# Sums of squares on two column halves of the TensorE array, ahead of the two MLPs

## The chip, the cores and the metric

One core of a Trainium2 chip runs the whole program. The metric is the device time of one execution in microseconds (us). TensorE (PE) multiplies, VectorE (DVE), ScalarE (ACT) and GpSimd (POOL) work element by element, and SyncE and ACT issue most of the DMAs. The engines run side by side and meet at semaphores.

## The reference, cut to what matters

The program is a two-layer encoder trunk over 16 learned and 1024 given tokens (1040 in all) of width 1024. Each layer adds a mixer (RG-LRU and gated linear attention heads) and then an MLP, each of them with an RMSNorm before it and one behind it.

```python
def rmsnorm(x, g):
    y = xf * lax.rsqrt(jnp.mean(xf * xf, axis=-1, keepdims=True) + EPS)
    return y.astype(x.dtype) * g
...
for l in range(DEPTH):
    mix = hybrid_mixer(rmsnorm(h, norm_mix_pre[l]), ...)
    h = h + rmsnorm(mix, norm_mix_post[l])
    ff = squared_relu_mlp(rmsnorm(h, norm_mlp_pre[l]), w_mlp_up[l], w_mlp_down[l])
    h = h + rmsnorm(ff, norm_mlp_post[l])
```

The change is in how `mean(xf * xf)` of the RMSNorm ahead of the MLP (norm_mlp_pre) is summed over the 1024 features.

## The kernel before, in words

**Layout.** Activations lie with the features on the 128 partitions, in KT = 8 feature tiles, and the tokens along the free axis. Layer 0 works on 3 blocks of 348 tokens (`FULL`, the last block is 344 wide in the weight products), layer 1 behind the mixer on 2 blocks of 512 (`LAST`). A *piece* is two feature tiles of one block: 12 pieces of 2 x 348 columns in layer 0, 8 pieces of 2 x 512 in layer 1. Four pieces (QT) make a block.

**Products.** Weights and activations are split into a high and a low part of type fp32r, and each product is three passes: high x high, high x low, low x high. Sums over the partitions are plain fp32 products with a matrix of ones, so that every output partition holds the sum. An fp32 product shows in the trace as two records of MATMUL, an fp32r pass as one.

**Where the change sits.** Behind the mixer, `update(l, 0, ...)` makes the new residual piece by piece. DVE scales and adds (L2050, L2061), ACT writes the high part of the piece scaled by the gain (L1421, called x_hi below) and its squares, both feature tiles at once, into a ring of three (`sq`, L1426), and DVE writes the low part (L2021, called x_lo below). TensorE follows in `first_pair`, which multiplies the first two weight units of the MLP (jobs J_MLP and J_MLP+1) with the pieces as they come. For each piece it does the high passes (L865), then `add_piece`, the two fp32 products of the piece's squares with ones (L852, L853) into a sum bank, then the low passes (L870). In the last block the second unit's passes are put off in part: its feature tiles 4 to 7 come after the last piece, 8 high passes and 4 low ones.

**What follows.** When the last piece of a block is summed, ACT takes the logarithm out of the sum bank (`log_mean`, L1407) and an exponential (`inv_root`, L1414), which gives 1/rms in `rs`. The norm's scale is applied behind the product: DVE's relu (L2443) multiplies the up projection's banks by `rs` and so needs all blocks of it. Only that relu frees the bank set of job J_MLP (`ps_free`, 3 banks in layer 0, 2 in layer 1), and the third unit (`unit_job`, L808) waits for this set. The two sum banks alternate from block to block, and a block's first sum waits until ACT has read the sum two blocks back (`take_sum_bank`). The sum of the norm behind the mixer (`row_sum`, L992) stands after piece 2 in layer 0 and after piece 1 in layer 1. The order of all of it is written out by hand, the same in each engine's program, and semaphores count pieces and sums. `acc` is the tile in which DVE adds up the squares of the mixer's output; it is free once L992 has read it.

Of the kernel before, what the change touches and what calls it, by code (L numbers as in the profile page):

```python
# [21 lines left out]
D = 1024  # L22
N_META, SEQ = 16, 1024
NT = N_META + SEQ
NB, BN = 3, 348
# [75 lines left out]
NX, QT = NB * KT // 2, KT // 2  # L101
# [157 lines left out]
def trunk_kernel(nc, x_in, w_units, w_zg, w_gates, w_decay, params, h_out):  # L259
# [6 lines left out]
    with ctx:  # L266
# [3 lines left out]
        def sem(name):  # L270
            return ctx.enter_context(nc.semaphore(name))
# [174 lines left out]
        def sq(t, n):  # L446
            return sq_last[n % SQ_RING][:, :, :] if t is LAST else sq_full[:, n % SQ_RING]
# [5 lines left out]
        def stream(dram, n, t):  # L453

            m, b = piece(n)
            return dram[m:m + 2, :, t.first + b * t.bn:t.first + (b + 1) * t.bn].rearrange("k p n -> p k n")

        def sum_bank(l, norm, b):

            return banks[:, 6 + sum_index(l, norm, b) % 2, 0:of_norm(l, norm).bn]  # L460
# [13 lines left out]
        x_hi, x_lo = sem("x_hi"), sem("x_lo")  # L474
        sq_h, sq_added, sq_read = sem("sq_h"), sem("sq_added"), sem("sq_read")
        sum_done, sum_read = sem("sum_done"), sem("sum_read")
        rs_ready = sem("rs_ready")
        banks_zeroed, branch_end = sem("banks_zeroed"), sem("branch_end")
        pad_zeroed, conv_step, xc_ready = sem("pad_zeroed"), sem("conv_step"), sem("xc_ready")
# [322 lines left out]
        def _(pe):  # L802
# [38 lines left out]
            def add_piece(l, norm, n, sbase):  # L841

                t, b, first, last = of_norm(l, norm), n // QT, n % QT == 0, n % QT == QT - 1
                if first:
                    take_sum_bank(l, norm, b)
                if sbase == 0:
                    pe.wait_ge(sq_added, n + 1)
                    nc.tensor.matmul(sum_bank(l, norm, b), ones[:, :], sq(t, n)[:, 0, :], start=first, stop=last)\
                        .then_inc(sum_done if last else sq_read, 1)
                    return  # L850
                pe.wait_ge(sq_h, sbase + n + 1)
                nc.tensor.matmul(sum_bank(l, norm, b), ones[:, :], sq(t, n)[:, 0, :], start=first, stop=False)  # L852
                nc.tensor.matmul(sum_bank(l, norm, b), ones[:, :], sq(t, n)[:, 1, :], start=False, stop=last)\  # L853
                    .then_inc(sum_done if last else sq_read, 1)

            def first_pair(l, norm, unit, j, slots, xbase, sbase, last_sum):

# [4 lines left out]
                def hi_passes(u, b, k, parts=(0, 1)):  # L862
                    w, lead = wslot(slots[u], k), lead_of(u, b)
                    for n in parts:
                        nc.tensor.matmul(ps(j + u, t=t)[:, b, lead:t.width(b)], w[n], xtile(k)[0][:, b * t.bn + lead:b * t.bn + t.width(b)],  # L865
                                         start=k == 0 and n == 0, stop=False)
# [42 lines left out]
                for n in range(2 if sbase == 0 else 0, t.pieces):  # L909
                    m, b = piece(n)  # L910
                    late = b == t.nb - 1

                    lag = [k - QT for k in (m, m + 1) if k >= QT] if late else [m, m + 1]
                    if n == 0:
                        pe.wait_ge(w_ready, l * COUNTED_UNITS + unit + 3)
                        take_set(l, j)
                    pe.wait_ge(x_hi, xbase + n + 1)
                    for k in (m, m + 1):
                        hi_passes(0, b, k)
                    if n == 0:  # L920
                        pe.wait_ge(w_ready, l * COUNTED_UNITS + unit + 1 + 3)
                        take_set(l, j + 1)
                    for k in lag:
                        hi_passes(1, b, k)
                    add_piece(l, norm, n, sbase)
                    pe.wait_ge(x_lo, xbase + n + 1)
                    for k in (m, m + 1):
                        first = lo_pass(0, b, k)
                    if n == t.pieces - 1:
                        first.then_inc(mm_done, 1)  # L930
                    for k in lag:
                        lo_pass(1, b, k)
                    if n == (2 if t is FULL else 1) and last_sum:
                        row_sum(*last_sum)
                for k in range(QT, KT):
                    hi_passes(1, t.nb - 1, k)
                for k in range(QT, KT):
                    ins = lo_pass(1, t.nb - 1, k)
                ins.then_inc(mm_done, 1)
# [47 lines left out]
            def row_sum(l, phase, b):  # L987

                norm = POST_MIX + 2 * phase
                take_sum_bank(l, norm, b)  # L990
                pe.wait_ge(acc_done, total(adds, l, phase) + whole_adds(l, phase) + (b + 1) * per_block(l, phase))
                nc.tensor.matmul(sum_bank(l, norm, b), ones[:, :], acc[:, projected_tokens(l, phase).cols(b)], start=True, stop=True)\  # L992
                    .then_inc(sum_done, 1)
# [409 lines left out]
        def _(act):  # L1403
            def log_mean(l, norm, b):

                act.wait_ge(sum_done, sum_index(l, norm, b) + 1)
                nc.scalar.activation(rs[:, of_norm(l, norm).cols(b)], sum_bank(l, norm, b), ACT.Ln, scale=1.0 / D, bias=eps[:, 0:1])\  # L1407
                    .then_inc(sum_read, 1)

            def inv_root(l, norm, b):  # L1410

# [14 lines left out]
                nc.scalar.activation(sq(t, n), Y[:, m:m + 2, t.cols(b)], ACT.Square).then_inc(sq_h, 1)  # L1426

            def last_sum(l, norm):
                log_mean(l, norm, of_norm(l, norm).nb - 1)
                inv_root(l, norm, of_norm(l, norm).nb - 1)  # L1430

# [35 lines left out]
            def update(l, phase, source, target):  # L1467
# [59 lines left out]
                if t is LAST:  # L1527
                    new_piece(1)
                    new_piece(2)
                    root(norm, 1)  # L1530
                    new_piece(3)
                    new_piece(4)
                    log_mean(l, norm + 1, 0)
                    new_piece(5)
                    new_piece(6)
                    inv_root(l, norm + 1, 0)
                    new_piece(7)
                else:
                    new_piece(1)
                    squares_of(2, first)  # L1540
                    if phase == 1:
                        root(norm, 1)
                        new_piece(2)
                    else:
                        new_piece(2)
                        root(norm, 1)
                    squares_of(2, second)
                    new_piece(3)
                    new_piece(4)
                    root(norm, 2)  # L1550
                    new_piece(5)
                    new_piece(6)
                    log_mean(l, norm + 1, 0)
                    for n in range(7, NX - 1):
                        new_piece(n)
                    log_mean(l, norm + 1, 1)
                    inv_root(l, norm + 1, 0)
                    inv_root(l, norm + 1, 1)
                    new_piece(NX - 1)

            for n in range(2):
                m, b = piece(n)
# [1278 lines left out]
```

## Time and profile before

| | us |
|---|---|
| median of 3 runs | 2210.37 (2210.19 to 2212.29) |
| the profiled execution, its own time | 2211.12 |
| its span in the trace | 2209.4 |
| TensorE busy in the span | 2186.9 (99%) |
| VectorE busy | 1640.6 (74%) |
| ScalarE busy | 899.8 (41%) |
| fp32 products with ones ahead of the MLPs | 40: 24 of 348 columns, 16 of 512 |

Busy times overlap, since the engines run side by side. The stretches with the pieces ahead of the MLPs are 433 to 472 us (layer 0) and 1539 to 1576 us (layer 1). A busy TensorE is one that has a product in flight; how closely the products follow each other is seen from the starts of their rows.

### The profile page before, as it was taken

What the parts mean: (1) busy time and instruction counts of PE and PEld (TensorE: products, weight loads), DVE (VectorE), ACT (ScalarE), POOL (GpSimd) and SP (SyncE); (2) the same over time, 40 slices, a digit from 0 to 9 for tenths busy, and PEclk for the clock granted to TensorE, in tenths of its full rate; (3) what the DMA queues carried; (4) which work ended last, traced back from release to release, by engine and by line L of the source; (5) the groups of instructions that cost most, each with busy time, mean ns of one, the idle gap of its engine ahead of it and who ended that gap; (6) DMA issues with size and microseconds to landing.
All of it is one profiled execution on the core that took longest, in us unless ns stands there. A gap on an engine that the chain in (4) does not pass through costs nothing.

```text
span 2209.4 us, 34577 instructions
## 1 busy us (share of the span) xinstructions
PE 2186.9 (99%) x13888; PEld 1990.1 (90%) x13888; DVE 1640.6 (74%) x1649; ACT 899.8 (41%) x1053; POOL 342.9 (16%) x195
## 2 busy tenths in 40 slices
PE   8999999999999999999999999999999999999998
PEld 7999989999999999999989999887788888888888
DVE  7788635576878877979687886354768779779897
ACT  4564424352433433333354653242524433433435
POOL 3333215112000000000313322151130000000000
PEclk9999999999999999999999999999999999999999
DMA  4111102255653654554341111022556544643744
GB/s 145 41 54 32 37 20 96 73 180 191 252 183 138 221 187 160 194 202 172 110 142 42 53 39 39 20 96 69 179 208 231 190 182 168 237 171 127 253 152 153
DMA packets 126928, 300.49 MB, mean 136 GB/s; under 512 B 9840, under 2 KB 29552, under 8 KB 126832
## 3 DMA queue, kind: packets, MB, share of 16 engines
q1 hardware_dynamic: 59568, 172.58, 21.9%
q10 hardware_dynamic: 67264, 126.55, 16.7%
q8 instruction: 70, 1.15, 0.2%
q14 instruction: 26, 0.21, 0.0%
HBM read 265.24 MB, written 33.85 MB: 135 GB/s over the span
## 4 chain that ended last, share of the span: by engine, by line
PE 87%; DVE 8%; ACT 2%; issue 2%; DMA 0%; POOL 0%; SPq 0%; DVEq 0%; ACTq 0%; POOLq 0%
PE banks L808 26%; PE banks L1142 23%; PE banks L1179 22%; PE banks L978 5%; PE banks L865 3%; DVE lr L2205 1%; PE banks L870 1%; PE banks L1279 1%; PE banks L853 1%; PE banks L852 1%; PE banks L1286 1%; PE banks L1256 1%; PE banks L1235 1%; PE banks L1294 1%; DVE xc L2234 1%
## 5 line engine op out<-in xcount | busy, mean ns | idle before, releaser
L808 PE MATMUL banks<-X,w_hl 128*128 128x348 f32 (+3 forms) x3264 | 556.9, 329 | 0.0
L808 PEld LDWEIGHTS banks<-X,w_hl 128*128 128x128 f32 x3264 | 522.8, 188 | 17.1 <-issue 3.0
L1142 PE MATMUL banks<-X,w_hl 128*128 128x260 f32 (+1 forms) x2268 | 363.4, 320 | 0.0
L1142 PEld LDWEIGHTS banks<-X,w_hl 128*128 128x128 f32 x2268 | 323.9, 188 | 34.1 <-DVE Y L2468 0.4
L1179 PE MATMUL banks<-sum_hi,w_hl 128*128 128x260 f32 (+1 forms) x1440 | 310.5, 320 | 0.0
L708 POOL TENSOR_SCALAR w_hl<-w_raw 128x1024 fp32r<-128x1024 f32 x59 | 69.5, 1178 | 1155.8 <-PE banks L1142 515.7
L1179 PEld LDWEIGHTS banks<-sum_hi,w_hl 128*128 128x128 f32 x1440 | 223.6, 188 | 21.1
L1179 PE MATMUL banks<-sum_lo,w_hl 128*128 128x260 f32 (+1 forms) x720 | 191.1, 320 | 0.0
L712 POOL TENSOR_TENSOR w_hl<-w_raw,w_hl 128x1024 fp32r<-128x1024 f32 x59 | 174.6, 2959 | 4.9
L1795 ACT ACTIVATE sum_hi<-hid 128x1040 fp32r<-128x1040 f32 (+1 forms) x72 | 76.8, 1066 | 200.1 <-PE banks L1179 200.1
L2537 DVE TENSOR_TENSOR Y<-banks,Y 128x520 f32<-128x520 f32 (+1 forms) x144 | 122.5, 872 | 21.6 <-PE banks L1179 20.8
L1179 PEld LDWEIGHTS banks<-sum_lo,w_hl 128*128 128x128 f32 x720 | 119.0, 188 | 10.6
L1761 ACT ACTIVATE w_hl<-r 128x1024 fp32r<-128x1024 f32 x76 | 80.2, 1055 | 113.5 <-PE banks L1179 55.2
L1179 PE MATMUL banks<-sum_hi,w_third 128*128 128x260 f32 (+1 forms) x576 | 125.7, 320 | 0.0
L1142 PE MATMUL banks<-X,w_third 128*128 128x260 f32 (+1 forms) x756 | 124.6, 321 | 0.1
L1142 PEld LDWEIGHTS banks<-X,w_third 128*128 128x128 f32 x756 | 108.4, 188 | 12.6 <-DMA X<-t_mem 1.3
L1776 ACT ACTIVATE hid<-banks 128x1040 f32<-128x1040 f32 (+1 forms) x56 | 57.9, 1033 | 143.4 <-PE banks L1142 143.2
L2485 DVE TENSOR_TENSOR w_hl<-w_raw,w_hl 128x1024 fp32r<-128x1024 f32 x52 | 63.6, 1223 | 52.4 <-ACT w_hl L1761 52.4
L2485 DVE TENSOR_TENSOR w_hl<-r,w_hl 128x1024 fp32r<-128x1024 f32 x76 | 92.7, 1220 | 7.2 <-ACT w_hl L1761 7.0
L1179 PEld LDWEIGHTS banks<-sum_hi,w_third 128*128 128x128 f32 x576 | 89.8, 188 | 8.4
L1780 ACT ACTIVATE hid<-hid 128x1040 f32<-128x1040 f32 (+1 forms) x56 | 59.9, 1069 | 91.1 <-DVE hid L2507 82.8
L2537 DVE TENSOR_TENSOR Z<-banks,Z 128x520 f32<-128x520 f32 (+1 forms) x108 | 91.7, 874 | 4.4 <-PE banks L1179 3.8
(271 smaller groups left out, 3706.9 us busy)
## 6 DMA issues: line engine op xcount, KB each, us to landing
w_raw<-w_units SPq DMA_DIRECT2D x142, 512.0 KB, 3.5
r<-w_units SPq DMA_DIRECT2D x88, 512.0 KB, 4.0
X<-t_mem ACTq DMA_DIRECT2D x52, 520.0 KB, 5.5
X<-t_mem ACTq DMA_DIRECT2D x52, 512.0 KB, 5.4
X<-t_mem SPq DMA_DIRECT2D x32, 520.0 KB, 5.6
X<-t_mem SPq DMA_DIRECT2D x32, 512.0 KB, 5.8
t_extra<-t_mem ACTq DMA_DIRECT2D x19, 520.0 KB, 4.4
t_extra<-t_mem ACTq DMA_DIRECT2D x19, 512.0 KB, 5.3
```

Of the source, the lines that this page charges most:

```text
L708: nc.gpsimd.tensor_scalar(slot[:, 0], w_raw[:, s], 1.0, 1.0, ALU.mult, ALU.mult).then_inc(w_rounded, 1)
L712: nc.gpsimd.tensor_tensor(slot[:, 1], w_raw[:, s], slot[:, 0].bitcast(f32), ALU.subtract).then_inc(w_ready, 1)
L808: ins = nc.tensor.matmul(out[:, b, lead:t.width(b)], wp, xp[:, b * t.bn + lead:b * t.bn + t.width(b)], start=first and n == 0, stop=last a ...
L865: nc.tensor.matmul(ps(j + u, t=t)[:, b, lead:t.width(b)], w[n], xtile(k)[0][:, b * t.bn + lead:b * t.bn + t.width(b)], start=k == 0 and n ...
L978: ins = nc.tensor.matmul(block_bank(j0, q)[:, 0:t.width(b)], wp, xp[:, t.used(b)], start=i == 0 and n == 0, stop=i == last_k and n == 2)
L1142: ins = nc.tensor.matmul(banks[:, first + b, 0:t.block], wp, xp[:, b * t.block:(b + 1) * t.block], start=opens and (half, kk, i) == (0, 0, ...
L1179: ins = nc.tensor.matmul(out[:, m + b, :], wp, xp[:, k, b * t.block:(b + 1) * t.block], start=k == 0 and i == 0, stop=k == 1 and i == 2)
L1761: nc.scalar.activation(wslots[W_SLOT[operand]][:, 0], r_first[:, :, :] if first else raws[raw], ACT.Copy).then_inc(wpart_hi, 1)
L1780: nc.scalar.activation(quarter(l, q), quarter(l, q), ACT.Square).then_inc(act_sq, 1)
L1795: nc.scalar.activation(sum_part(l, sum_hi, part), source, ACT.Copy).then_inc(xpart_hi, 1)
L2485: V.tensor_tensor(slot[:, 1], r_first[:, :, :] if first else raws[W_RAW[operand]], slot[:, 0].bitcast(f32), ALU.subtract).then_inc(wpart_r ...
L2537: ins = V.tensor_tensor(to, part_banks(l, job), to, ALU.add)
```

## The change

In `add_piece`, for the norm ahead of the MLP alone, the two products of a piece no longer use the whole array one after the other. Each uses 64 of its 128 columns (`ones[:, rows]`): the first feature tile's squares are summed into partitions 0 to 63 of the sum bank, the second tile's into partitions 64 to 127. When a block's four pieces are through, the bank holds two half sums. ACT copies it to `acc` (`copy_halves`), and TensorE adds the halves by a whole fp32 product with ones (`whole_sum`). Each of the two is then in it 64 times, which the scale of the logarithm takes out (`repeated`). In TensorE's program `whole_sum` of a block stands after piece 2 of the next block in layer 0 (pieces 6 and 10), after piece 1 of it in layer 1 (piece 5), and for the last block between the last 8 high and the last 4 low passes of the second unit. ACT's order is shifted to fit.

```diff
@@ add_piece (TensorE)
                 pe.wait_ge(sq_h, sbase + n + 1)
+                if norm == PRE_MLP:
+                    for half in range(2):
+                        rows = slice(64 * half, 64 * half + 64)
+                        ins = nc.tensor.matmul(sum_bank(l, norm, b)[rows], ones[:, rows], sq(t, n)[:, half, :], start=first, stop=last,
+                                               skip_group_check=True)
+                    ins.then_inc(halves_done if last else sq_read, 1)
+                    return
                 nc.tensor.matmul(sum_bank(l, norm, b), ones[:, :], sq(t, n)[:, 0, :], start=first, stop=False)
                 nc.tensor.matmul(sum_bank(l, norm, b), ones[:, :], sq(t, n)[:, 1, :], start=False, stop=last)\
                     .then_inc(sum_done if last else sq_read, 1)
+
+            def whole_sum(l, norm, b):
+
+                pe.wait_ge(halves_copied, halves_before(l, norm, b) + 1)
+                nc.tensor.matmul(sum_bank(l, norm, b), ones[:, :], acc[:, of_norm(l, norm).cols(b)], start=True, stop=True).then_inc(sum_done, 1)
@@ first_pair (TensorE)
                     if n == (2 if t is FULL else 1) and last_sum:
                         row_sum(*last_sum)
+                    if norm == PRE_MLP and n % QT == (2 if t is FULL else 1) and n > QT:
+                        whole_sum(l, norm, n // QT - 1)
                 for k in range(QT, KT):
                     hi_passes(1, t.nb - 1, k)
+                if norm == PRE_MLP:
+                    whole_sum(l, norm, t.nb - 1)
                 for k in range(QT, KT):
                     ins = lo_pass(1, t.nb - 1, k)
@@ log_mean (ScalarE)
+                repeated = 64 if norm == PRE_MLP else 1
                 act.wait_ge(sum_done, sum_index(l, norm, b) + 1)
-                nc.scalar.activation(rs[:, of_norm(l, norm).cols(b)], sum_bank(l, norm, b), ACT.Ln, scale=1.0 / D, bias=eps[:, 0:1])\
+                nc.scalar.activation(rs[:, of_norm(l, norm).cols(b)], sum_bank(l, norm, b), ACT.Ln, scale=1.0 / (D * repeated), bias=eps[:, 0:1])\
                     .then_inc(sum_read, 1)
+
+            def copy_halves(l, norm, b):
+
+                act.wait_ge(halves_done, halves_before(l, norm, b) + 1)
+                nc.scalar.activation(acc[:, of_norm(l, norm).cols(b)], sum_bank(l, norm, b), ACT.Copy).then_inc(halves_copied, 1)
@@ last_sum (ScalarE)
+                if norm == PRE_MLP:
+                    copy_halves(l, norm, of_norm(l, norm).nb - 1)
                 log_mean(l, norm, of_norm(l, norm).nb - 1)
                 inv_root(l, norm, of_norm(l, norm).nb - 1)
@@ update, layer 1 (ScalarE)
                     new_piece(4)
-                    log_mean(l, norm + 1, 0)
+                    copy_halves(l, norm + 1, 0)
                     new_piece(5)
                     new_piece(6)
+                    log_mean(l, norm + 1, 0)
+                    new_piece(7)
                     inv_root(l, norm + 1, 0)
-                    new_piece(7)
...
```

TensorE's program at one piece of layer 0 (the first piece of the stretch; `w_out_87` and `w_out_88` are the slots of the first two weight units), before:

```order
L865 MATMUL banks<-X,w_out_88 128x348 x4
L852 MATMUL banks<-sq,ones 128x348
L853 MATMUL banks<-sq,ones 128x348
L870 MATMUL banks<-X,w_out_87 128x348 x2
L870 MATMUL banks<-X,w_out_88 128x348 x2
```

and after the change:

```order
L882 MATMUL banks<-X,w_out_88 128x348 x4
L860 MATMUL banks<-sq,ones 64x348 x2
L887 MATMUL banks<-X,w_out_87 128x348 x2
L887 MATMUL banks<-X,w_out_88 128x348 x2
```

The two whole products have become two of 64 columns; the passes on either side stand as they did.

TensorE's program at the end of the same stretch, from the last piece to the third unit (`w_hl`), before:

```order
L865 MATMUL banks<-X,w_out_88 128x344 x4
L852 MATMUL banks<-sq,ones 128x348
L853 MATMUL banks<-sq,ones 128x348
L870 MATMUL banks<-X,w_out_87 128x344 x2
L870 MATMUL banks<-X,w_out_88 128x344 x2
L865 MATMUL banks<-X,w_out_88 128x344 x8
L870 MATMUL banks<-X,w_out_88 128x344 x4
L808 MATMUL banks<-X,w_hl 128x348 x2
```

and after the change:

```order
L882 MATMUL banks<-X,w_out_88 128x344 x4
L860 MATMUL banks<-sq,ones 64x348 x2
L887 MATMUL banks<-X,w_out_87 128x344 x2
L887 MATMUL banks<-X,w_out_88 128x344 x2
L882 MATMUL banks<-X,w_out_88 128x344 x8
L871 MATMUL banks<-acc,ones 128x348
L887 MATMUL banks<-X,w_out_88 128x344 x4
L813 MATMUL banks<-X,w_hl 128x348 x2
```

The product that completes the last block's sum now stands behind 12 more passes than before (2 + 2 + 8), with 4 passes left behind it instead of 16.

ScalarE's program at the same place, from the high part of the last piece (piece 11), before:

```order
L1421 ACTIVATE X<-Y,par 128x348 x2
L1426 ACTIVATE sq<-Y 128x696
L1487 DMA h_mid<-Y 128x2x348
L1407 ACTIVATE rs<-banks,eps 128x348
L1414 ACTIVATE rs<-rs 128x348
L1906 ACTIVATE x_scaled<-Y,par 128x1040 x2
```

and after the change:

```order
L1448 ACTIVATE X<-Y,par 128x348 x2
L1453 ACTIVATE sq<-Y 128x696
L1516 DMA h_mid<-Y 128x2x348
L1429 ACTIVATE rs<-banks,eps 128x348
L1441 ACTIVATE rs<-rs 128x348
L1435 ACTIVATE acc<-banks 128x348
L1429 ACTIVATE rs<-banks,eps 128x348
L1441 ACTIVATE rs<-rs 128x348
L1951 ACTIVATE x_scaled<-Y,par 128x1040 x2
```

The logarithm and exponential of the middle block have moved behind the last piece, and the copy of the last block's half sums (`acc<-banks`) stands ahead of its logarithm.

## Rows read from the trace of the kernel before

**Rows 1.** The page: busy time by engine, and TensorE's granted clock in 40 slices.
```profile
PE 2186.9 (99%) x13888; PEld 1990.1 (90%) x13888; DVE 1640.6 (74%) x1649; ACT 899.8 (41%) x1053; POOL 342.9 (16%) x195
...
PEclk9999999999999999999999999999999999999999
```

**Rows 2.** The page: the chain that ended last, by engine.
```profile
PE 87%; DVE 8%; ACT 2%; issue 2%; DMA 0%; POOL 0%; SPq 0%; DVEq 0%; ACTq 0%; POOLq 0%
```

**Rows 3.** Timeline, PE, layer 0: start us, duration us, then the merged group.
```profile
437.07 1.44 PE L865 MATMUL banks<-X,w_out 128*128 128x348 f32 x8
...
440.16 1.44 PE L865 MATMUL banks<-X,w_out 128*128 128x348 f32 x8
```

**Rows 4.** Chain in order of time, one fp32 product of each layer: start us, us.
```profile
439.09 0.58 PE banks L853 x2
...
1571.65 0.86 PE banks L853 x2
```

**Rows 5.** Timeline, PE, two long rows of fp32r passes, one for each layer.
```profile
471.61 8.65 PE L808 MATMUL banks<-X,w_hl 128*128 128x348 f32 x53
...
1576.06 22.39 PE L808 MATMUL banks<-X,w_hl 128*128 128x512 f32 x96
```

**Rows 6.** Timeline, PE, the products on 32-column quarters (128*32), and what follows.
```profile
41.76 3.70 PE L1358 MATMUL banks<-Y,zg_w 128*32 128x348 f32 x48 [0.17 <-DVE xb L1963]
45.39 0.43 PE L808 MATMUL banks<-X,w_hl 128*128 128x348 f32 x1
```

**Rows 7.** Timeline, PE, into and out of products on 64-column halves (104*64).
```profile
249.22 0.80 PE L808 MATMUL banks<-X,w_hl 128*128 128x344 f32 x4
249.95 1.09 PE L1235 MATMUL banks<-v_tok,keys_t 104*64 104x128 f32 x16
250.98 0.64 PE L1223 MATMUL banks<-ident,ki 128*104 128x128 f32 x4
...
275.71 0.82 PE L1235 MATMUL banks<-v_tok,keys_t 104*64 104x128 f32 x12
276.46 1.71 PE L808 MATMUL banks<-X,w_hl 128*128 128x348 f32 x9
```

**Rows 8.** Timeline, PE, ACT and DVE, the end of layer 0's stretch.
```profile
466.49 1.41 PE L865 MATMUL banks<-X,w_out 128*128 128x344 f32 x8
467.74 0.75 PE L852 MATMUL banks<-sq,ones 128*128 128x348 f32 x2
...
469.11 0.56 ACT L1407 ACTIVATE rs<-banks,eps 128x348 f32<-128x348 f32 x1 [4.28 <-PE banks L853]
469.69 0.49 ACT L1414 ACTIVATE rs<-rs 128x348 f32<-128x348 f32 x1
...
470.22 2.64 DVE L2443 SCALAR_TENSOR_TENSOR T<-banks,rs 128x1044 f32<-128x1044 f32 x2 [4.96 <-ACT rs L1414]
```

**Rows 9.** Timeline, PE, ACT and DVE, the end of layer 1's stretch.
```profile
1568.79 2.00 PE L865 MATMUL banks<-X,w_out 128*128 128x512 f32 x8
1570.63 1.02 PE L852 MATMUL banks<-sq,ones 128*128 128x512 f32 x2
...
1572.55 0.69 ACT L1407 ACTIVATE rs<-banks,eps 128x512 f32<-128x512 f32 x1 [5.13 <-PE banks L853]
...
1573.93 1.23 DVE L2443 SCALAR_TENSOR_TENSOR T<-banks,rs 128x1024 f32<-128x1024 f32 x1 [6.01 <-ACT rs L1414]
```

**Rows 10.** Timeline, PE and DVE, inside layer 1's stretch, and one DVE row of layer 0.
```profile
1548.25 1.02 PE L992 MATMUL banks<-acc,ones 128*128 128x512 f32 x2
1561.18 1.09 PE L865 MATMUL banks<-X,w_out 128*128 128x512 f32 x4
...
1550.69 1.23 DVE L2050 TENSOR_TENSOR Y<-Y,rs 128x1024 f32<-128x1024 f32 x1 [1.50 <-ACT rs L1414]
1561.10 1.41 DVE L2021 SCALAR_TENSOR_TENSOR X<-Y,par,X 128x512 fp32r<-128x512 f32 x2
...
460.67 1.06 DVE L2021 SCALAR_TENSOR_TENSOR X<-Y,par,X 128x348 fp32r<-128x348 f32 x2
```

More of the change, by code:

```diff
@@ L456, in stream, with halves_before @@
             return dram[m:m + 2, :, t.first + b * t.bn:t.first + (b + 1) * t.bn].rearrange("k p n -> p k n")
+        def halves_before(l, norm, b):
+            return NB * l + b
         def sum_bank(l, norm, b):
@@ L476, in trunk_kernel @@
         sum_done, sum_read = sem("sum_done"), sem("sum_read")
+        halves_done, halves_copied = sem("halves_done"), sem("halves_copied")
         rs_ready = sem("rs_ready")
@@ L1550, in update @@
                     root(norm, 2)
[L1551 to L1559, printed above, removed]
+                    if phase == 0:
+                        new_piece(5)
+                        new_piece(6)
+                        copy_halves(l, norm + 1, 0)
+                        new_piece(7)
+                        new_piece(8)
+                        log_mean(l, norm + 1, 0)
+                        new_piece(9)
+                        new_piece(10)
+                        copy_halves(l, norm + 1, 1)
+                        inv_root(l, norm + 1, 0)
+                        new_piece(NX - 1)
+                        log_mean(l, norm + 1, 1)
+                        inv_root(l, norm + 1, 1)
+                    else:
+                        new_piece(5)
+                        new_piece(6)
+                        log_mean(l, norm + 1, 0)
+                        for n in range(7, NX - 1):
+                            new_piece(n)
+                        log_mean(l, norm + 1, 1)
+                        inv_root(l, norm + 1, 0)
+                        inv_root(l, norm + 1, 1)
+                        new_piece(NX - 1)
             for n in range(2):
```

## The prediction, made before the changed kernel ran

> **What bounds the kernel now.** I read the page's busy times first: TensorE is busy for 2186.9 of 2209.4 us at the full granted clock, the 2.4 GHz level, in every slice [rows 1], and the chain that ended last is 87% TensorE [rows 2]. So the change counts by what it does to TensorE's stream in two stretches of about 40 us, and by whether that stream must wait at their ends. The timeline of these stretches comes next. In layer 0 a piece takes 3.09 us, from 437.07 to 440.16 [rows 3]: 12 fp32r passes and two fp32 products. An fp32 product costs 0.585 us there and 0.86 in layer 1, by the steps of the chain [rows 4]. An fp32r pass costs (8.65 - 0.32) / 52 = 0.160 us in layer 0 and (22.39 - 0.40) / 95 = 0.231 in layer 1 (0.32 and 0.40 being one pass alone) [rows 5]; within the pieces 8 passes take 467.74 - 466.49 = 1.25, so 0.157 each [rows 8]. TensorE waits for nobody in the stretches. It is about to at their ends: in layer 0 the last sum is out at 469.1, ACT's two steps run to 470.2, DVE's first relu, half of 2.64 us or 1.25 alone, ends at about 471.47 [rows 8], and the third unit starts at 471.61 [rows 5]. That is sum to restart 2.5 us, and TensorE's own 16 passes behind that sum's stream (468.91 + 16 x 0.157) end just 0.2 us before it. In layer 1 DVE is through at 1573.93 + 1.23 = 1575.16 [rows 9], while TensorE's own passes last until 1576.06 [rows 5]: 0.9 us of slack.
>
> **What the change removes.** Two 64-column products side by side take the time of one. The trace has that: 16 records of 64-column products in 1.09 us [rows 7]. One after the other at the 0.109 us that a step has there (0.82 - 0.27 over 5 steps of the 12-record row) they would take 1.74; in pairs 0.87 and the latency. On quarters of the array and all 128 rows it holds too: 48 records in 3.70 us are 12 steps of 0.29 [rows 6]. So a piece saves 0.585 us (layer 0) or 0.86 (layer 1) before costs.
>
> **What a visit to the halves costs.** Going in: four whole passes from 249.22 at 0.157 end at 249.85, but the first pair starts at 249.95, 0.10 late, and the pairs then need 1.09 - 0.27 = 0.82 us for seven steps of 0.11, 0.05 too long [rows 7]. Coming out: the last pair of the 12-record row starts at 275.71 + 0.82 - 0.27 = 276.26, the next product is due at 276.37 and comes at 276.46, 0.09 late, and its nine passes take 1.71 where 8 steps of 0.16 and 0.32 make 1.60: 0.11 more. Together 0.35 us a visit. The quarters' exit agrees: 45.39 is 0.12 later than 41.76 + 12 x 0.2925, and the first pass lasts 0.43 instead of 0.32 [rows 6]. Bounds: 0.20 if the late entry was only a wait for data, 0.40 by the quarters' exit. I take 0.35, whose rows are of this very tile width.
>
> The Trainium skill, "TensorEngine Tiling (Array Packing)", Key Properties, says that changing the tiling mode drains TensorE; it gives no price. The trace agrees, with the 0.35 us above. The same page's Theoretical Speedup table gives up to 2x for two column halves; taken alone, without the drain, that is the second rival below.
>
> So a piece saves 0.585 - 0.35 = 0.235 us in layer 0 and 0.86 - 0.35 = 0.51 in layer 1.
>
> **What it adds.** Five whole products with ones (three of 0.585, two of 0.86) and five copies on ACT. A copy is priced by its nearest row, the logarithm out of the same bank, 0.56 or 0.69 us [rows 8, 9], between 0.5 and 0.8. ACT is 41% busy [rows 1] and each copy is made long before it is wanted. The tightest is the last: the copy is there 0.6 us after the half sums, and TensorE has 12 passes (1.9 us) in between. So the copies cost nothing; without that cover each would cost its 0.6.
>
> **Layer 0, step by step.** When the last piece starts TensorE is ahead by 11 x 0.235 less two whole sums, 2.59 - 1.17 = 1.4 us, so at 465.1. DVE keeps ahead of that: the low parts of piece 10 end at 460.67 + 1.06 = 461.7 [rows 10], and TensorE wants them 4 passes and a whole sum before 465.1, at 463.9; those of piece 11 need 1.07 more and are wanted at 467.3. No stall. Then come 8 passes (1.25), the halves (0.585 + 0.35), 12 passes (1.88) and the whole sum until it is out (0.75, the two records of such a product [rows 8]): the sum is out at 465.1 + 4.8 = 469.9 instead of 469.1. Behind it stands the same logarithm, exponential and relu, 2.5 us. Of TensorE's own work only 4 passes are left, which end 0.46 us behind the sum (0.585 + 0.63 - 0.75), so it waits about 2.1 us, and the third unit starts 0.85 us LATER than before. The queue behind the wait is the whole MLP: TensorE's program is in order, and no later idle time in it is large enough to give this back.
>
> **Layer 1, step by step.** Savings of 0.51 a piece bring TensorE up to DVE. DVE's start on the second block hangs on the row sum at 1548.25, behind piece 1 [rows 10], which comes 1.0 us sooner; DVE follows from 1550.69 on, without a gap, so all its later steps come 1.0 sooner: the low parts of piece 5 end at 1561.10 + 1.41 - 1.0 = 1561.5. TensorE starts piece 5 at 1561.18 - 5 x 0.51 = 1558.6 and wants them 0.93 + 0.86 + 0.35 later, at 1560.8. Stall 0.7. The lead at the last piece is then 7 x 0.51 - 0.86 - 0.7 = 2.0: start 1566.8 instead of 1568.79 [rows 9]. Then 8 passes (1.84), the halves (1.21), 12 passes (2.77), the whole sum until it is out (1.02): 1573.6, where 1572.5 was before, so 1.1 later. DVE's relu then ends at 1576.3, and the unit starts at about 1576.4, with the hop, against 1576.06: +0.35 us.
>
> **The sum.** +0.85 + 0.35 = +1.2 us. The profiled execution took 2211.12 in all, span 2209.4; it would be 2212.3. It lies 0.75 above the median of the runs, so the median goes from 2210.37 to 2211.6. In short, 20 visits at 0.35 (7.0) and five whole sums (3.5) use up all of the 13.9 us saved but 3.4; the stall at piece 5 takes 0.7, and 3.9 go to the late sum, for which TensorE idles 2.1 us in layer 0, where it idled 0.2 before, and 2.0 in layer 1. With a visit of 0.20 layer 0 comes out at -0.95 and layer 1, where DVE then bounds more, at about -0.5: 2208.9. With 0.40 it is +1.0 more: 2212.6.
>
> **Rival: the late sum costs nothing.** If something else released the third unit, TensorE's own passes would decide: layer 0 gains 12 x 0.235 - 3 x 0.585 = 1.07 and the 0.2 us of waiting, layer 1 gains 8 x 0.51 - 2 x 0.86 - 0.7 = 1.7, together -2.9: 2207.5. Against it: before, the third unit started 0.14 us behind the end of the relu, just as if it waited for it [rows 5, 8]. For it: layer 1 has 0.9 us of slack today [rows 5, 9].
>
> **Rival: no switching cost.** If the weight loads hid the switch, TensorE would run into DVE. In layer 0 piece 11's low parts could be there at 461.73 + 1.07 = 462.8 [rows 10], then 12 passes and the whole sum: out at 465.4, 3.6 us sooner. In layer 1 the low parts of the last piece would come at about 1566.9 (end 1567.9 today), the sum at 1570.7 and the unit at 1573.5: 2.6 sooner. Total -6.2: 2204.2. Against it: every exit in rows 6 and 7.
>
> **Rival, slower: the halves do not run side by side** for 128 rows, 64 columns and 348 or 512 fp32 columns, say because both stream from the same ring slot into one bank. Then a visit costs 0.35 and saves nothing. Layer 0's sum is out 12 x 0.585 later than forecast (+7.0), layer 1's 8 x 0.86 later less the 0.7 stall (+6.2): 14.4 us over before, 2224.8. It decides once less than half of the overlap is there: the change is then over 4.4 us slower. Against it: rows 6 (128 rows) and 7 (64 columns). That the change does nothing is no case; its instructions are other ones.
>
> **How the numbers follow.** Forecast 0.83, late sum free 0.07, no switching cost 0.04, halves in a row or a dearer switch 0.06. A measurement of this kernel can tell 0.2%, 4.4 us, from no change. The forecast and the first rival lie within it: same 0.89; the second is faster: 0.05 with a tail of mixtures; slower 0.06. The range, 2208.5 to 2214.3, holds the bounds of the visit and about 1 us of spread between runs on either side; it leaves out the rivals.
>
> **What would show it.** Pieces of layer 0 about 2.85 us apart instead of 3.09; 64-column records in pairs less than 0.02 us apart, with the next pass 0.09 late; the last sum out near 470 and 1573.6, a wait of TensorE of about 2 us ahead of each third unit, released by DVE's relu, and a short stall before low passes in layer 1's piece 5. Pieces still 3.0 us or more apart, or third units that start without a wait, would make it wrong.

## The result, and the profile after

The changed kernel takes 2214.84 us (median of 21 runs, 2213.05 to 2218.3), the kernel before beside it 2211.97 (21 runs, 2210.19 to 2213.57): ratio 1.0016, 95% interval 1.001 to 1.0021. It is slower, by less than the 0.2% set as the bound, and the time lies 0.5 us above the predicted range. The profiled execution took 2213.96 us, 2.84 more than before's 2211.12.

From the page: busy time by engine, the granted clock in 40 slices and the chain that ended last, to be laid beside [rows 1, 2].

```profile
PE 2184.2 (99%) x13898; PEld 1980.9 (90%) x13898; DVE 1641.5 (74%) x1649; ACT 902.2 (41%) x1058; POOL 342.2 (15%) x195
...
PEclk9999999999999999999999999999999999999999
...
PE 86%; DVE 9%; ACT 2%; issue 2%; DMA 1%; POOL 0%; SPq 0%; DVEq 0%; ACTq 0%; POOLq 0%
```

TensorE is busy for 2.7 us less and the span is 2.8 us longer, so it idles 5.5 us more. Three waits shown below, of 1.90, 0.79 and 1.87 us, make 4.6 of that; the rest lies before and behind the stretches (the start-up was 1.35 us longer, 0.6 of them idle). The timeline of PE in layer 0 (start us, duration us, group) shows a piece [rows 3] and the end of the stretch [rows 5, 8]:

```profile
435.03 1.74 PE L882 MATMUL banks<-X,w_out 128*128 128x348 f32 x8
...
438.18 1.44 PE L882 MATMUL banks<-X,w_out 128*128 128x348 f32 x8
439.54 0.81 PE L860 MATMUL banks<-sq,ones 128*64 128x348 f32 x4
440.28 0.90 PE L887 MATMUL banks<-X,w_out 128*128 128x348 f32 x4
441.02 1.43 PE L882 MATMUL banks<-X,w_out 128*128 128x348 f32 x8
...
469.24 1.42 PE L882 MATMUL banks<-X,w_out 128*128 128x344 f32 x8
470.50 0.75 PE L871 MATMUL banks<-acc,ones 128*128 128x348 f32 x2
470.82 1.07 PE L887 MATMUL banks<-X,w_out 128*128 128x344 f32 x4
473.78 6.43 PE L813 MATMUL banks<-X,w_hl 128*128 128x348 f32 x39 [1.90 <-DVE T L2488]
```

A piece takes 441.02 - 438.18 = 2.84 us instead of 3.09. The four records of the half products are together done in 0.81 us, so both halves do run at once. The last sum is out at 471.25 (470.50 + 0.75), TensorE runs out of passes at 471.9 and then stands for 1.90 us. ACT's logarithm and exponential and DVE's relu fill that time:

```profile
471.28 0.55 ACT L1429 ACTIVATE rs<-banks,eps 128x348 f32<-128x348 f32 x1 [2.21 <-PE banks L871]
471.87 0.49 ACT L1441 ACTIVATE rs<-rs 128x348 f32<-128x348 f32 x1
...
472.39 2.40 DVE L2488 SCALAR_TENSOR_TENSOR T<-banks,rs 128x1044 f32<-128x1044 f32 x2 [7.97 <-ACT rs L1441]
```

The same timeline in layer 1: the start of the stretch, the stall at piece 5, and the end [rows 5, 9].

```profile
1541.11 2.20 PE L882 MATMUL banks<-X,w_out 128*128 128x512 f32 x8
...
1561.73 1.08 PE L860 MATMUL banks<-sq,ones 128*64 128x512 f32 x4
1563.59 0.73 PE L887 MATMUL banks<-X,w_out 128*128 128x512 f32 x2 [0.79 <-DVE X L2066]
...
1566.97 1.08 PE L860 MATMUL banks<-sq,ones 128*64 128x512 f32 x4
...
1569.02 2.00 PE L882 MATMUL banks<-X,w_out 128*128 128x512 f32 x8
1570.95 1.08 PE L860 MATMUL banks<-sq,ones 128*64 128x512 f32 x4
...
1574.84 1.02 PE L871 MATMUL banks<-acc,ones 128*128 128x512 f32 x2
1575.30 1.48 PE L887 MATMUL banks<-X,w_out 128*128 128x512 f32 x4
1578.65 6.74 PE L813 MATMUL banks<-X,w_hl 128*128 128x512 f32 x28 [1.87 <-DVE T L2488]
```

TensorE waits 0.79 us for the low parts of piece 5 and 1.87 us ahead of the third unit. To compare across kernels I measure each stretch from its first pass to its third unit. Three rows of the kernel before in the same view, the two starts and one piece of layer 1:

```profile
433.68 1.74 PE L865 MATMUL banks<-X,w_out 128*128 128x348 f32 x8
...
1539.08 2.20 PE L865 MATMUL banks<-X,w_out 128*128 128x512 f32 x8
...
1566.14 1.02 PE L852 MATMUL banks<-sq,ones 128*128 128x512 f32 x2
```

Before: 471.61 - 433.68 = 37.93 and 1576.06 - 1539.08 = 36.98. After: 473.78 - 435.03 = 38.75 and 1578.65 - 1541.11 = 37.54. That is +0.82 and +0.56, **+1.38 us** together. The same differences in all traces (stretches, and the time before, between and behind them; us):

```
kernel            to L0    L0    between    L1   to end    span
before           433.68  37.93  1067.47  36.97  633.31  2209.36
changed          435.03  38.75  1067.32  37.55  633.58  2212.23
again            433.80  38.75  1067.02  37.53  634.06  2211.17
after_look       434.60  38.75  1067.83  37.54  633.74  2212.47
after_third      433.57  38.75  1068.65  37.54  634.76  2213.27
last_sum_sooner  433.38  37.81  1067.65  36.15  633.35  2208.36
last_block_whole 434.59  37.22  1067.76  35.82  633.05  2208.42
pairs_last_whole 434.10  35.81  1067.90  35.34  633.57  2206.71
pairs_again      433.58  35.80  1067.51  35.31  634.11  2206.30
late_sum_alone   433.02  39.79  1067.55  39.00  633.35  2212.72
late_sum_look    433.50  39.81  1068.65  39.00  633.97  2214.93
latest_sum       433.19  40.43  1067.82  39.92  635.11  2216.46
latest_again     434.54  40.43  1068.84  39.91  635.25  2218.98
filled           434.01  38.75  1068.82  37.55  636.43  2215.56
filled_layer0    434.00  38.75  1068.84  37.54  635.55  2214.68
filled_layer1    434.66  38.75  1067.59  37.56  633.83  2212.38
latest_filled    434.59  40.43  1068.57  39.91  633.62  2217.13
```

The stretches of equal kernels repeat to 0.03 us; start-up (the time to L0), in which the change does nothing, scatters over 2 us. So the stretches tell what an edit does in its place, and the medians whether something is added elsewhere.

### The profile page after: what moved, and what is told of

The parts are those of the page before. It is cut to its first block, busy times and chain, and to the rows that moved or that the text cites. A ratio compares the mean times of both kernels' runs of the same rounds, so it can differ in the third digit from the quotient of the medians.

```text
span 2212.2 us, 34602 instructions
## 1 busy us (share of the span) xinstructions
PE 2184.2 (99%) x13898; PEld 1980.9 (90%) x13898; DVE 1641.5 (74%) x1649; ACT 902.2 (41%) x1058; POOL 342.2 (15%) x195
## 4 chain that ended last, share of the span: by engine, by line
PE 86%; DVE 9%; ACT 2%; issue 2%; DMA 1%; POOL 0%; SPq 0%; DVEq 0%; ACTq 0%; POOLq 0%
PE banks L813 26%; PE banks L1163 22%; PE banks L1200 22%; PE banks L999 5%; PE banks L882 2%; DVE lr L2250 1%; PE banks L887 1%; PE banks L1300 1%; PE banks L1307 1%; PE banks L1277 1%; PE banks L1256 1%; PE banks L1315 1%; PE banks L860 1%; DVE xc L2279 1%; DVE qi L2389 0%
```

## The experiments

My theory: pieces save what the visit leaves, the late sum costs more, and the rest of the extra time is not in the stretches. Rivals: the visit is dearer than forecast; the late sum costs nothing; all of the rest is the scatter of the median.

### again, after_look and after_third: the changed kernel once more

No edit.

> The changed kernel once more, for the clock and time of each run beside runs of the kernel before. By the trace the two stretches ahead of the MLPs cost +1.4 us (0.82 in layer 0, 0.56 in layer 1); 1.35 us more of the profiled difference lie in the first 16 us, where the first weights landed 0.5 us later and the clock rose 5.7 instead of 4.0 us after the first product. Theory A, the start and the clock's rise fall by chance and alike for both kernels: here the median comes out 1 to 2 us over before, and the profile's start differs from the last one. Theory B, the change itself costs about 3 us, be it through code that loads differently or through the clock, which falls when TensorE idles 2 us: the median is again 2.5 to 3.5 us over before.

> The changed kernel once more, for the same question: in a run of 0.998 or less the clock falls behind one of the two idle stretches of 1.9 us (theory) or only at the end (rival).

> The changed kernel once more, unfilled, beside the filled one: +2.6 to 2.9 in the median, some runs at 0.997, by the theory; by the rival it does not differ from the filled one.

`again` took 2214.04 (11 runs; ratio 1.0012, 1.0003 to 1.0021), `after_third` 2214.26 (11 runs; the same ratio and interval), `after_look` 2214.2 (one run). The ratio of 1.0016 repeats within its interval, and `again` lies 2.58 us over the kernel before on its chip, where theory A had 1 to 2 and theory B 2.5 to 3.5: the change itself costs more than its stretches. `after_look` was a run at .999 without a fall of the clock and left its question open. Only `after_third` shows something new. Stretches behind its two idle times, TensorE's records in brackets and the granted clock as PEclk:

```profile
core 0: us, PE busy (x) PEld busy (x) DVE busy (x) ACT busy (x) POOL busy (x), PEclk, DMA share, GB/s
473.80:477.00 3.20, 3.20 (x13) 3.20 (x12) 1.89 (x2) 3.14 (x4) 0.00 (x0) 0.50 0.00 0
1579.80:1583.00 3.20, 3.20 (x9) 2.53 (x8) 1.75 (x2) 3.14 (x4) 0.00 (x0) 0.50 0.00 0
```

and the same stretches of the first profile of the changed kernel:

```profile
473.80:477.00 3.20, 3.20 (x20) 3.20 (x21) 1.42 (x2) 3.17 (x4) 0.00 (x0) 1.00 0.00 0
1579.80:1583.00 3.20, 3.20 (x16) 2.58 (x15) 1.60 (x2) 3.14 (x4) 0.00 (x0) 1.00 0.00 0
```

At 0.50, the 1.2 GHz level, TensorE has fewer passes in flight: 13 where it had 20, and 9 where it had 16. A window's count takes in passes that reach over its ends, so the price is better read from the long rows of `after_third`'s timeline:

```profile
472.32 9.85 PE L813 MATMUL banks<-X,w_hl 128*128 128x348 f32 x51 [1.90 <-DVE T L2488]
...
1578.51 11.76 PE L813 MATMUL banks<-X,w_hl 128*128 128x512 f32 x43 [1.87 <-DVE T L2488]
```

At the rate of the first profile's rows above, (6.43 - 0.32) / 38 = 0.161 us and (6.74 - 0.40) / 27 = 0.235 us a pass, they would take 8.4 and 10.3 us. So each fall costs 1.5 us, 3.0 in all. TensorE had stood 1.90 and 1.87 us just before. The page's row of 40 slices doesn't show it, since a slice is 55 us long. The mean clock of a run hints at it: this one has 0.997, the other three traces 0.999. Sorted by it, all 44 runs of the changed kernel have medians of 2213.52 (23 runs at .999), 2214.84 (9 at .998) and 2216.23 (12 at .997): 1.3 and 2.7 us over those at .999, near what one fall and two falls cost. The runs of the kernel before whose clock is known have 2212.10 (75 runs at .999) and 2212.01 (23 at .998), and **none of 98 is at .997**. A run at .998 says less: below, two traces at .998 have one fall (`latest_sum`, `filled_layer0`), and three have none (`last_sum_sooner`, `late_sum_look`, `latest_filled`), but their clock is low for the last 7.5 to 7.8 us of the program, where it is 5.0 us in the kernel before.

### last_sum_sooner: the last sum behind one high pass group

```diff
                 for k in range(QT, KT):
                     hi_passes(1, t.nb - 1, k)
-                if norm == PRE_MLP:
-                    whole_sum(l, norm, t.nb - 1)
+                    if norm == PRE_MLP and k == QT:
+                        whole_sum(l, norm, t.nb - 1)
```

> The changed kernel with the last block's whole sum placed 6 passes sooner, behind the first 2 of the 8 last high passes. Theory (late sum): the sum is out 6 x 0.157 = 0.94 us sooner in layer 0 and 6 x 0.231 = 1.39 in layer 1, TensorE idles about 1.0 and 0.5 us instead of 1.9 and 1.87, and the time falls by 2.3 us against the changed kernel, to 0.9 under before by the stretches. If the relu or the rest did not hang on this sum, nothing changes: 0 against the changed kernel.

2210.35 us (11 runs), ratio 0.9993 (0.9984 to 1.0002): no slower than before. By the stretches it is 0.94 us shorter than before, as expected (0.9). Its median is 3.7 below that of `again` on the same chip, where 2.3 was expected: more than the stretches goes with the waits. Its waits ahead of the third units, PE:

```profile
471.18 9.13 PE L813 MATMUL banks<-X,w_hl 128*128 128x348 f32 x56 [0.96 <-DVE T L2488]
...
1575.01 10.22 PE L813 MATMUL banks<-X,w_hl 128*128 128x512 f32 x43 [0.48 <-DVE T L2488]
```

The sum comes 6 passes sooner (6 x 0.157 = 0.94 us, and 6 x 0.231 = 1.39), and the third unit comes 0.94 and 1.39 us sooner. So the time of the third unit hangs on this sum, pass by pass, and the rival of a free late sum falls. No run is at .997.

### last_block_whole: the last block's squares as before

```diff
-                if norm == PRE_MLP:
+                if norm == PRE_MLP and b < t.nb - 1:
                     for half in range(2):
...
-                if norm == PRE_MLP:
-                    whole_sum(l, norm, t.nb - 1)
```

> Halves for all blocks but the last of each layer, whose pieces keep the two whole products and need no second one. Theory (late sum): the waits of 1.9 us ahead of both third units go, TensorE reaches the last piece 8 x 0.24 - 2 x 0.585 = 0.75 us sooner in layer 0 and 4 x 0.51 - 0.86 = 1.18 sooner in layer 1, and the restart follows: -1.9 us against before, -3.3 against the changed kernel by the stretches. If the halves themselves (tile switches, two streams from one ring slot) were what costs, most of the loss would stay and it would be 0 to +1 us. If the 2 us of idle TensorE lower the clock in some runs, this kernel has no such runs and lies 4 us or more under the changed one.

2210.15 us (11 runs), 0.9994 (0.9985 to 1.0003). TensorE doesn't wait ahead of either third unit:

```profile
471.81 8.50 PE L813 MATMUL banks<-X,w_hl 128*128 128x348 f32 x52
...
1575.37 9.90 PE L813 MATMUL banks<-X,w_hl 128*128 128x512 f32 x42
```

The stretches are 1.86 us shorter than before, where 1.9 was expected; the median is 1.3 below before's, and 3.9 below the changed kernel's on the same chip (`again`), where 4 or more was expected. No run is at .997.

### pairs_last_whole and pairs_again: two pieces' halves in one visit

On top of `last_block_whole`:

```diff
-                    add_piece(l, norm, n, sbase)
+                    if norm != PRE_MLP or late:
+                        add_piece(l, norm, n, sbase)
+                    elif n % 2 == 1:
+                        add_piece(l, norm, n - 1, sbase)
+                        add_piece(l, norm, n, sbase)
```

> Halves for all blocks but the last, and the squares of two pieces summed in one visit to the halves. Against the kernel with the last block whole it makes 6 visits fewer: 4 in layer 0, 2 in layer 1. Theory (a visit costs 0.35 us): 2.1 us less than that kernel, 4.0 less than before by the steps (8 x 0.585 - 4 x 0.35 - 2 x 0.585 = 2.1 and 4 x 0.86 - 2 x 0.35 - 0.86 = 1.9). Rival (the visit's cost is hidden, or the pieces wait for ACT, whose ring of squares is now read later): no difference to the kernel with the last block whole.

> The kernel pairs_last_whole once more: the last piece's squares by whole products, the halves of two pieces in one visit, so 8 visits fewer than the changed kernel and no late sum. Expected from its first time (0.9984 of the kernel before) 2208.9 to 2209.1 us, 3 us under the kernel before, with runs at a mean clock of .998 or .999 alone. The rival is that its gain was within the scatter: a ratio whose interval holds 1.

2208.95 (11 runs; 0.9984, 0.9975 to 0.9993), then 2208.34 on another chip (11 runs; 0.9981, 0.9972 to 0.999): faster than both kernels, by 3.45 and 4.47 us against the kernel before on the same chip, at most 0.3%. The stretches are 3.75 and 3.79 us shorter than before, where 4.0 was expected. The second expectation miscounts: the kernel has 6 visits where the changed one has 20, so 14 fewer. `pairs_again`, the eight records of two pieces on PE:

```profile
437.17 1.39 PE L860 MATMUL banks<-sq,ones 128*64 128x348 f32 x8
438.49 0.91 PE L887 MATMUL banks<-X,w_out 128*128 128x348 f32 x4
```

The second piece adds 1.39 - 0.81 = 0.58 us, a whole product's time for a piece's two, and no visit of its own. The 6 visits that are gone save 1.41 us in layer 0 (4 visits) and 0.48 in layer 1 (2) over `last_block_whole`, so 0.35 and 0.24 a visit, 0.31 on the mean. In layer 1 this doesn't make the visit cheaper: a piece there saves 0.51 of 0.86 us in the changed kernel, which again leaves 0.35. Of the two visits removed the first saves 0.33 us (from the first pass to the row sum 8.16 us became 7.83) and the second 0.20 (from there to piece 4 8.83 became 8.63), where the 8 high passes ahead of the squares take 0.1 us longer than they did, for a reason that is not shown. The rival of a dearer visit falls.

### late_sum_alone, late_sum_look and latest_sum, latest_again: the late sum without the halves

In the kernel before, the last piece's two whole products behind the 8 high passes:

```diff
-                    add_piece(l, norm, n, sbase)
+                    if norm != PRE_MLP or n < t.pieces - 1:
+                        add_piece(l, norm, n, sbase)
...
                     hi_passes(1, t.nb - 1, k)
+                if norm == PRE_MLP:
+                    add_piece(l, norm, t.pieces - 1, sbase)
```

and in the `latest` pair behind the 4 low passes as well.

> The kernel before, with whole products everywhere, but with the two products of the last piece's squares moved behind the 8 last high passes. No halves, no copies. Theory (late sum): the sum is out at 466.5 + 1.25 + 0.63 + 1.26 + 1.33 = 471.0 in layer 0, the third unit restarts 2.5 later, +1.9 us; in layer 1 the sum is at 1575.3, restart at 1578.1, +2.0. Together +3.9 us over before, with about 2 us of idle TensorE twice. If idle stretches of that length lower the clock later in some runs, it is more than that in the median, 5 us and up, and the granted clock is below 0.999 in these runs as it is in runs of the changed kernel.

> The kernel with only the late sum once more, to see where its granted clock falls. Theory: in a run of 0.998 or less there is a stretch at the 1.2 GHz level behind 470 or behind 1577 us, where TensorE idles 2 us, of a few us, and each product in it takes twice as long. Rival: the clock only falls sooner at the program's end, where TensorE has little to do.

> The kernel before with whole products, and the two products of the last piece's squares behind all the other passes (8 high and 4 low). By the steps the third units restart at 474.1 and 1579.0, +2.5 and +2.9 us, +5.4 in all, with TensorE idle 2.7 and 2.9 us. Theory (idle lowers the clock): as in the run with the sum 4 passes sooner, whose median was 1.4 us over its steps, most runs are 1.5 us or more over +5.4, median 7 us or more over before, granted clock 0.998 or less. Rival (only the steps): median +5.4 +- 1.

> The kernel with the latest sum once more, unfilled, beside the filled one on the same chip: +7 us and more in the median, most runs at 0.997, where the steps make +5.4. If it comes out at +5.4 here, the earlier extra was the chip's and not the idle stretches'.

`late_sum_alone` took 2216.75 (11 runs; 1.0024, 1.0015 to 1.0033), the look 2216.66; `latest_sum` 2219.85 (5 runs; 1.0037, 1.0023 to 1.0051), `latest_again` 2220.84 (5 runs; 1.0041, 1.0027 to 1.0054). Their stretches are longer than before by 3.89 and 5.45 us (3.9 and 5.4 expected), and the medians by 5.3 and 7.5 to 9. In `latest_sum` TensorE waits 2.54 and 2.79 us, and behind the second:

```profile
1582.20:1585.40 3.20, 3.20 (x9) 2.55 (x8) 1.44 (x3) 3.14 (x4) 0.00 (x0) 0.50 0.00 0
```

Nine passes, again at 0.50. This trace has one fall and a mean clock of .998. `latest_again` has a fall behind both waits, and all five of its runs are at .997. The traces of `late_sum_alone` and of its look show no fall, though two of its 11 runs are at .997. Here the expectation missed: the look was a run at .998, its clock fell only at the program's end (the rival), and its trace is 1.1 us longer between the stretches at full clock, in small steps whose cause is open. So the 1.4 us by which this kernel's median exceeds its stretches are not shown to be the clock's. Without any half products, a longer idle time of TensorE does bring the half clock in more of the runs (3 and then 5 of 5 at .997, where it was 12 of 44 and 2 of 11 behind waits of 1.87 to 1.91 us).

### filled, latest_filled, filled_layer0, filled_layer1: work in the wait

Products of ones of 128 columns whose result nobody reads, 8 in the changed kernel and 12 in the latest kernel, in each wait or in one layer's (`and l == 0`, `and l == 1`):

```diff
+                if norm == PRE_MLP:
+                    pe.wait_ge(sum_read, sum_index(l, norm, t.nb - 2) + 3)
+                    for i in range(8):
+                        nc.tensor.matmul(sum_bank(l, norm, t.nb - 2)[:, 0:128], ones[:, :], ones[:, :], start=True, stop=True)
```

> The changed kernel, and in the waits ahead of both third units TensorE does 8 small products of ones with ones (128 columns, 0.21 us each, 1.7 us in all) whose result nobody reads. The waits themselves stay, so the stretches cost the same +1.4 us. Theory (idle lowers the clock in some runs): no run is below 0.998 in granted clock, and the median is +1.4 over before instead of +2.6 to 2.9. Rival (the extra has nothing to do with idle TensorE): the median stays at +2.6 to 2.9 and runs at 0.997 remain.

> The kernel with the latest sum (whole products, sum behind all other passes), its two waits of 2.7 and 2.9 us filled with 12 such products (2.6 us). By the steps still +5.4 us. Theory: median +5.4, no run at 0.997. Rival: +7.5 as before, with runs at 0.997.

> The changed kernel with 8 small products of ones in TensorE's wait ahead of the third unit in layer 0 only (their result is read by nobody). In the kernel filled, which had them in both layers, no granted clock fell in the middle of the trace, but the time rose by 3 us over the changed kernel and its trace had waits of TensorE for loads of X (1.55 us at 557.60, 1.44 us in the last unit groups). Theory A, the added products bring on the later wait for the load of their own layer: this kernel shows a wait of more than 1 us near 557 and none beyond 0.6 in the last groups, and takes 1.2 to 2 us more than the changed kernel's 2213.5 at an undisturbed clock, 2215 us. Rival B, those waits were chance of one profile: no wait for a load over 0.6 us, time between 2213.2 and 2214.2. The fall of the clock behind layer 1's stretch is still open to it in part of the runs, so the runs at a mean clock of .999 are to be compared.

> The same small products in layer 1 only. Theory A: no wait near 557, waits for loads or for the accumulator over 1 us in the last groups, time 1 to 2 us over the changed kernel's 2213.5, so 2215. Rival B: no such wait, 2213.2 to 2214.2. If each of the two kernels adds about half of filled's 3.6 us over the undisturbed runs of the changed kernel, the cost of the filling is settled and the miss of filled says nothing against the clock theory; if both take 2213.5, filled's time stays open.

The clock part came for the most part: `latest_filled` has no run of seven at .997 where `latest_again` beside it had five of five, `filled` one of 11 where none was expected (at 2222.31 us, the longest of all and unexplained), and neither trace has a fall. The time part missed. `filled` took 2217.12 (11 runs; 1.0025, 1.0016 to 1.0034), 4 us more than forecast, though its stretches are to 0.01 us those of the changed kernel. TensorE in `filled`, far behind the stretches:

```profile
557.60 3.13 PE L1167 MATMUL banks<-X,w_third 128*128 128x260 f32 x24 [1.55 <-DMA X<-t_mem]
...
2129.80 1.42 PE L1167 MATMUL banks<-X,w_third 128*128 128x512 f32 x5 [1.10 <-DMA X<-t_mem]
...
2170.89 0.67 PE L1017 MATMUL banks<-acc,ones 128*128 128x256 f32 x2 [1.52 <-DVE acc L2033]
```

Three waits, 4.2 us, that the changed kernel has not. `latest_filled` (2218.66, 7 runs; 1.0028, 1.0017 to 1.0039) has the first of them too, 1.16 us; it took 7.0 us over the kernel before, where 5.4 was expected, and 2.2 less than `latest_again` beside it. One layer at a time then tells more. `filled_layer0` took 2216.45 (11 runs; 1.0017, 1.0008 to 1.0026), 3.6 over the kernel before, with the wait at 557 again:

```profile
557.21 3.13 PE L1167 MATMUL banks<-X,w_third 128*128 128x260 f32 x24 [1.14 <-DMA X<-t_mem]
```

The same trace holds the plainest comparison, the stretches behind its filled wait in layer 0 and its idle wait (1.87 us, until 1579.14) in layer 1:

```profile
474.50:477.70 3.20, 3.20 (x22) 3.20 (x21) 2.16 (x2) 3.06 (x3) 0.00 (x0) 1.00 0.00 0
1580.10:1583.30 3.20, 3.20 (x9) 2.46 (x9) 1.44 (x3) 3.14 (x4) 0.00 (x0) 0.50 0.00 0
```

Full clock behind the filled one, half clock behind the idle one, in one execution, whose mean clock is .998.

`filled_layer1` took 2214.3 (11 runs; 1.0009, 1.0 to 1.0018), **1.49 us over the kernel before** on its chip, beside 1.40 in the stretches. One of its runs is at .997; its wait in layer 0 is idle as before. It has none of the three waits, and its wait ahead of the third unit is filled:

```profile
1576.53 1.95 PE L964 MATMUL banks<-ones 128*128 128x128 f32 x16
1578.56 6.74 PE L813 MATMUL banks<-X,w_hl 128*128 128x512 f32 x28
```

So filling layer 0 brings a wait for a load in three traces of three, where none of the other 14 has it, and filling layer 1 costs nothing. Theory A is right for layer 0, though 2216.45 us is more than its 2215, and wrong for layer 1. Why products at 471 us should make a load late at 557 is open, and so are the two late waits of `filled`, which neither half of it repeats.

## Why the prediction was wrong

**Right, by steps.** A piece of layer 0 saves 0.25 us (0.235 forecast), of layer 1 0.51 (1570.63 - 1566.14 = 4.49 before, 1570.95 - 1566.97 = 3.98 after). Layer 0's last sum comes 0.80 us later in its stretch (0.8), TensorE waits 1.90 us for it (2.1), and the third unit comes 0.82 later (0.85, where the forecast's own steps add up to 0.80). In layer 1 piece 5 stalls for 0.79 (0.7), and the wait is 1.87 (2.0). The third unit comes 0.56 later instead of 0.35: the lead at the last piece is 1.8 us, not 2.0 (1568.79 - 1539.08 less 1569.02 - 1541.11). The stretches sum to +1.4 where the forecast had +1.2. The visit at 0.35 is confirmed by the pieces of both layers and by its removal in layer 0 (0.35; in layer 1 0.24 came back). The Trainium skill, "TensorEngine Tiling (Array Packing)", Key Properties, has a drain at each change of mode, which agrees. Its "up to 2x" for two column halves holds for the products alone.

**Wrong, the step "so the median goes from 2210.37 to 2211.6".** It took the median of three runs for the kernel's time. Of 21 runs beside the changed kernel it is 2211.97, 1.6 us more; the profiled execution's own 2211.12 stood nearer. That is half of the 3.24 us of error and says nothing on the change.

**Wrong, "It would be 2212.3", as if an idle TensorE cost only its idle time.** The forecast had the two waits of 2 us and priced them at their length. What stands behind them can run at the 1.2 GHz level, for 1.5 us more in each layer in `after_third`. In the first 21 runs the nine at .999 have a median of 2213.52, 1.55 over the kernel before, near the 1.4 of the stretches. The other twelve raise it to 2214.84, 1.32 more. With 1.6 of the base and 0.2 of the stretches that makes 3.1 of 3.24. That the idle time is what brings the fall is shown on three sides: more idle time without halves has more of it, kernels with waits under 1 us or none (before, `last_sum_sooner`, `last_block_whole`, the pairs) have no run of 142 at .997, and filling the wait takes the fall away in the traces. Counted over all 17 traces, the clock fell behind 6 of 18 idle waits of 1.87 us and more, behind none of 6 filled ones, and at none of the 10 places with a shorter wait or none. Mean clocks alone would show less, since one fall can leave .998; but in the kernel before the runs at .998 are no longer than those at .999. Filling layer 1's wait, without side effect, gives the time of the stretches alone (+1.49), though layer 0's stays idle. The share of each of the two layers in a median is not settled, since the mean clock doesn't tell which fell.

The Trainium skill, "TensorE: Matmul & The Clock Gate", Part 1, says that the gate sets the rate by how busy TensorE has lately been, and that equal kernels meet it in another phase from run to run. The page tells the second of a kernel's start. This case agrees, and shows it in the middle: behind the same waits one trace of the changed kernel in four has the half clock. I had read [rows 1], full clock in every slice, as if it would stay so.

**The rivals.** The late sum is not free (`last_sum_sooner`), switching is not free (`pairs_last_whole`), the halves do run side by side (0.81 us for four records).

## What to carry to other kernels

A saving inside a pipeline is worth what it does to the last item: here the 3.4 us saved in the pieces were lost to one sum of each layer moved behind 12 passes, so leave the last block as it was and batch what needs a mode switch. A wait of about 2 us that a change gives to a busy TensorE is to be priced above its length, with a chance that the passes behind it run at the half clock for a few us; look for it in the mean clock of each run and then in short stretches of a trace, not in the page's slices. A median of three runs is no base for a forecast to 0.1%.

## What the runs showed of the hardware

- Changing from whole products to two 64-column halves and back costs 0.35 us at 348 and at 512 columns by the steps of the pieces (six visits removed gave back 1.89 us), and further pieces in the same visit nothing more (0.58 us for a piece's two products, the time of one whole product).
- Behind idle times of TensorE of 1.87 us and more the granted clock fell to 0.50 in some executions (1.5 us lost each time) and in others of the same kernel not at all: 6 of 18 such waits in the traces. Behind 0.96 us, and behind waits filled with small products, it was not seen.
- Small products added in layer 0's wait (16 records in 1.95 us, 24 in 2.84) went with a wait of 1.1 to 1.6 us for a DMA some 85 us later in three traces of three, with no cause found.
